# Weights of a two-layer decoder trunk: one 1 MB transfer for two neighbouring ring slots in place of two of 512 KB

## The reference, cut to what matters

```
for l in range(DEPTH):                       # DEPTH = 2
    h = _rmsnorm(x, attn_norm[l])
    x = x + _hybrid_mixer(h, ..., w_in[l], ..., w_kv_b[l], ..., w_branch[l], w_out[l])
    h = _rmsnorm(x, ffn_norm[l])
    gate, up = jnp.split(h @ w_gate_up[l], 2, axis=-1)
    x = x + (jax.nn.silu(gate) * up) @ w_down[l]
```

## Time and profile before

| what | value |
|---|---|
| median of three runs | 2885.08 us (2885.07 to 2885.09) |
| the profiled execution's own time | 2884.71 us |
| its span, first to last instruction | 2882.9 us |
| PE busy | 2875.4 us, 12964 matmuls |
| DVE busy | 1823.1 us |
| ACT busy | 1339.0 us |
| POOL busy | 648.2 us |
| transfers on SP's queue | 540.54 MB |

### The profile page before, as it was taken

How to read it: one execution, slowest core, us unless ns; L and a number is a source line. 1 busy time by engine, 2 the same in 40 slices (tenths; PEclk the granted TensorE clock), 3 DMA queues, 4 the chain that set the end, 5 groups by cost and what they waited for, 6 DMA issues and landing times.

```text
span 2882.9 us, 35147 instructions
## 1 busy us (share of the span) xinstructions
PE 2875.4 (100%) x12964; PEld 2381.4 (83%) x12964; DVE 1823.1 (63%) x2223; ACT 1339.0 (46%) x1570; POOL 648.2 (22%) x1033
## 2 busy tenths in 40 slices
PE   9999999999999999999999999999999999999999
PEld 8888888888888888888888888888888888888887
DVE  7589866687655555545575898656775555555554
ACT  5445554554444444444444455455544444344443
POOL 0025224144122312300000242231441213213000
PEclk9999999999999999999999999999999999999999
DMA  7666666775666666666666666666766666666665
GB/s 247 183 185 195 202 186 189 232 235 190 192 192 194 194 190 195 193 194 192 193 193 176 196 190 197 191 189 228 238 191 194 191 194 192 193 193 194 193 194 170
DMA packets 291293, 567.35 MB, mean 197 GB/s; under 512 B 18985, under 2 KB 24945, under 8 KB 291185
## 3 DMA queue, kind: packets, MB, share of 16 engines
q1 hardware_dynamic: 283888, 540.54, 61.9%
q10 hardware_dynamic: 7296, 25.44, 2.7%
HBM read 551.23 MB, written 14.68 MB: 196 GB/s over the span
## 4 chain that ended last, share of the span: by engine, by line
PE 94%; POOL 2%; DVE 2%; issue 1%; ACT 0%; DMA 0%; ACTq 0%; SPq 0%; DVEq 0%
PE acc L456 61%; PE acc L461 30%; POOL small L387 2%; PE acc L503 1%; DVE w_lo L1197 1%; PE acc L501 1%; DVE nat L1197 0%; DVE small L1197 0%; ACT w_hi L807 0%; PE acc L514 0%; PE acc L494 0%; PE acc L509 0%; DVE small L1215 0%; DMA w_raw<-in_w_in_dram 0%; PE acc L515 0%
## 5 line engine op out<-in xcount | busy, mean ns | idle before, releaser
L1197 DVE TENSOR_TENSOR w_lo<-w_raw,w_hi 128x1024 fp32r<-128x1024 f32 x1024 | 1259.9, 1234 | 1013.4 <-ACT w_hi L807 1008.8
L807 ACT ACTIVATE w_hi<-w_raw 128x1024 fp32r<-128x1024 f32 x1024 | 1084.5, 1060 | 1480.1 <-PE acc L461 1447.6
L456 PE MATMUL acc<-w_hi,opa_hi 128*128 128x512 f32 (+1 forms) x2364 | 930.7, 394 | 0.6 <-ACT w_hi L807 0.6
L456 PE MATMUL acc<-w_hi,opa_lo 128*128 128x512 f32 (+1 forms) x2364 | 918.0, 388 | 0.0
L456 PE MATMUL acc<-w_hi,opb_hi 128*128 128x512 f32 x1728 | 672.9, 389 | 0.1
L456 PE MATMUL acc<-w_hi,opb_lo 128*128 128x512 f32 x1728 | 672.3, 389 | 0.0
L461 PE MATMUL acc<-w_lo,opa_hi 128*128 128x512 f32 (+1 forms) x2364 | 629.3, 388 | 0.0
L456 PEld LDWEIGHTS acc<-w_hi,opa_hi 128*128 128x128 f32 x2364 | 444.0, 188 | 93.8 <-issue 6.4
L461 PEld LDWEIGHTS acc<-w_lo,opa_hi 128*128 128x128 f32 x2364 | 443.1, 188 | 90.9 <-DVE w_lo L1197 0.4
L456 PEld LDWEIGHTS acc<-w_hi,opa_lo 128*128 128x128 f32 x2364 | 444.1, 188 | 87.6
L461 PE MATMUL acc<-w_lo,opb_hi 128*128 128x512 f32 x1728 | 461.8, 389 | 0.0
(11 more groups left out here) (188 smaller groups left out, 1136.3 us busy)
## 6 DMA issues: line engine op xcount, KB each, us to landing
w_raw<-in_w_gate_up_dram SPq DMA_DIRECT2D x352, 512.0 KB, 4.4
w_raw<-in_w_in_dram SPq DMA_DIRECT2D x336, 512.0 KB, 3.7
w_raw<-in_w_down_dram SPq DMA_DIRECT2D x176, 512.0 KB, 4.4
w_raw<-in_w_branch_dram SPq DMA_DIRECT2D x64, 512.0 KB, 4.6
w_raw<-in_w_out_dram SPq DMA_DIRECT2D x64, 512.0 KB, 4.3
gate_store<-nat ACTq DMA_DIRECT2D x24, 512.0 KB, 3.8
arena<-gate_store ACTq DMA_DIRECT2D x24, 512.0 KB, 5.5
w_raw<-in_w_kv_b_dram SPq DMA_DIRECT2D x16, 512.0 KB, 4.3
```

The costliest lines, as they stand in the source:

```text
L456: pe.matmul(bank(pair, t, width), op[j][:, kt + k, t * P:(t + 1) * P], w_hi[:, s, k, 0:width], start=(first and k == 0 and j == 0), stop=F ...
L807: return act.activation(out, in_, ACT.Copy, scale=scale)
L1197: return dve.tensor_tensor(out, a, b, op)
```

## The change

After the first eight units, each load brings two units: for an even slot SP waits until both slots are free (`lo_ready` for the second of them, unit `m + 1 - 4`) and issues one transfer of 1 MB into both; for an odd slot it issues nothing. `hi` of either unit waits on the semaphore of the even slot. Nothing else is changed.

```
             def unit(n, m, w, l, u, col, width=N):
+                count = 1 if n + m < UB else 2
                 slot = m % RING
-
-                sp.wait_ge(lo_ready, lo_count(n, m - RING))
+                if slot % count:
+                    return
+
+                sp.wait_ge(lo_ready, lo_count(n, m + count - 1 - RING))
                 view, per = w
-                sp.dma_start(raw[:, slot:slot + 1, :, 0:width],
-                             view[:, l * per + u:l * per + u + 1, :, col:col + width]).then_inc(raw_landed[slot], 16)
+                sp.dma_start(raw[:, slot:slot + count, :, 0:width],
+                             view[:, l * per + u:l * per + u + count, :, col:col + width]).then_inc(raw_landed[slot], 16)
...
             def hi(n, nq, m):

                 s = m % RING
-                act.wait_ge(raw_landed[s], nq + 16 * (m // RING + 1))
+                alone = isinstance(n, int) and n + m < UB
+                act.wait_ge(raw_landed[s if alone else s - s % 2], nq + 16 * (m // RING + 1))
                 act.wait_ge(unit_done, n + (m + 1))
                 copy(w_hi[:, s], raw[:, s]).then_inc(hi_ready, 1)
```

## The result

| | median us | lowest and highest | runs |
|---|---|---|---|
| before | 2885.09 | 2885.07 to 2885.43 | 4 |
| after | 2920.24 | 2919.34 to 2921.22 | 4 |

The ratio is 1.0122, with an interval of 1.0109 to 1.0134: slower by 35.15 us, where 14.4 were forecast, and above the range. The profiled execution took 2921.22 us, 36.5 more than that of before.

A forecast was written before the change was run, and what follows sets the result against it. The prediction took PE's matmuls as the bound (busy 2875.4 of 2882.9 us). Terms 5.9 + 5.7 + 1.0 + 1.7 = 14.3 us on 2884.71 gave 2899.0, adjusted to 2899.4 and stated as 2899.5 us; range 2893 to 2916.

The forecast's parts named there:

- direction: Whole kernel: slower than 2890.9 us, given 0.90 over the cases; the forecast time was 0.50% slower.
- block 6: PE stops at `pair_scores`, waiting for copies queued behind late `hi` 56: 5.9 us in the first layer, 5.7 in the second.
- the steady state costs nothing: Projections, gate/up and down: 4.1 us of lateness meets 4.1 of landing cover and 6.9 more in the ring; PE loses nothing.
- matmuls held up by writes: Faster rival, 0.04: pairs free matmuls from transfers' writes, winning 24.6 us; against it, unit times stay 2.72 us throughout 400 us.
- The rival with more stops: Stops elsewhere, as in output projection transposes: 2909 to 2925 us, 10 to 25 beyond the 14.3 sum; chance 0.22.
- the ring has 11 us of cover: Argument against more stops: between 11 us of cover in the ring and 4.1 of lateness there is mostly room.
- the clock: PE's idling in block 6 may bring slow matmuls: 0 to 3.4 us, taken as 1.7 for one of two stops.
- The rule of the Trainium skill weighed there: Idle PE falls to half rate until busy again; by it both block 6 stops pay, 1.7 us more in the sum.
- The start: First pair, units 8 and 9, lands late and DVE has no pause until `lo` 12: 1.0 us, between 0.1 and 2.
- the smaller stop: Rival, 0.08: 1 MB lands as soon as 512 KB, block 6 stops 4.5 and 4.3 us; 2891 to 2894.5 us.
- The rate rule of the Trainium skill: SP's transfers: gather to 1 MiB or more for 75% of peak rate; the prediction answered that no rate is short here.

The follow-up runs named there:

- e5: Changed kernel with all pairs, but in block 6 ACT's three `pair_sb` copies stand ahead of `hi` of unit 56: 2915.81 us, 1.0107 to before.
- e3: Kernel before with the pair's later wait kept, each pair issued as two 512 KB transfers with semaphores of their own: 2909.51 us, 1.0082 to before.
- e4: Pairs only from unit 256 of each layer on (gate/up and down projections), the others loaded as before: 2885.20 us, 0.9999 to before.
- e10: Pairs only in units 184 to 223 of each layer (branches and first output projection block), single loads elsewhere: 2899.41 us, 1.0049 to before.
- e7: Changed kernel plus 48 unused 128-column matmuls on PE ahead of its block 6 wait in `pair_scores`, both layers: 2918.27 us, 1.0116 to before.
- e9: Kernel before with only units 56 and 57 of each layer paired, plus 48 unused matmuls ahead of PE's `pair_scores` wait: 2897.98 us, 1.0046 to before.
- e8: Changed kernel with units 56, 57 and 184 to 223 of each layer loaded singly, all other pairs kept: 2898.58 us, 1.0044 to before.
- e1: Changed kernel with only units 56 and 57 of each layer loaded singly again: 2912.91 us, 1.0093 to before.
- e12: Pairs only in units 58 to 183 of each layer (end of input projection, attentions), single loads elsewhere: 2894.77 us, 1.0034 to before.

## Why the prediction was wrong, and where it was right

**Right: direction, and block 6.** It named the chain SP, DVE, ACT, PE and put 5.9 and 5.7 us on it; the waits are 5.76 and 5.8. It added nothing for what comes behind them, and up to unit 183 only 0.6 us came, both layers together. Issue to `hi` was taken as 5.00 and took 4.94. e5 shows that the chain goes through the copies' place, e3 that the second half counts 1.2 of it.

**Right: the steady state costs nothing,** The earlier trace rows against e4. So does the argument against matmuls held up by writes.

**Wrong, the step that decided: the output projection was left out of the sum.** The rival with more stops, into whose 2909 to 2925 us the result falls, named it: the transposes at line 494 wait without cover, 0.8 us each, up to 4.1 more each. They waited 3.7 more each, with 3.9 of clock behind them, and e10 measures the part with all that hangs on it at 14.4 us. The argument against, that the ring has 11 us of cover, holds for `hi` on its way to PE. The merge doesn't stand in the ring. It stands on DVE behind a `lo`, at the end of a way through DVE, POOL, ACT and DVE, and a wait of 0.8 us says that this way had no cover. A link that already waits passes on all of a delay, and should have stood in the sum by the same working as `pair_scores`, at 2.72 + 1.36 each, giving 8 more. That this is near the 3.7 measured is in part luck: the lateness comes in a block earlier, at `lo` 208, and the loads there take longer than the working has (7.2 us from issue to `hi` 208).

**Wrong, a size: the clock.** Taken as 1.7 us for one of two stops, with 3.4 as the upper bound. The clock fell at all four stops. Block 6 alone lost 2.4 + 2.7 = 5.1, above the bound: I had taken what 3.78 us of matmuls at the start lost, but in the stretch at half the clock from 163.09 to 169.92 PE works for 5.2 us, and half of this is 2.6. How much is lost varies, from 1.4 to 2.7 us for a stop in after. The rule of the Trainium skill weighed there (TensorE: Matmul & The Clock Gate, "The two states you'll see") is borne out by this trace: when PE starts again after each stop of 4.5 to 5.8 us, the granted clock is at the lower level.

**Wrong, smaller sizes.** The start was 2.3 us, not 1.0; `hi` 8 started at 32.23, 0.2 us later than forecast once the 0.4 us that this execution lost before its first unit is taken off, so that pair came nearly as forecast. The step that failed is that DVE would have no pause from there to `lo` 12: `hi` of units 10 and 11 waited 4.21 us for the next pair and started at 38.44, DVE waited for it, and `lo` 12 started at 46.91, 3.5 us later than before's 43.42 where 1.3 were forecast. Beyond the stops 5.8 us came in small pieces, most of them in the branches, where I had none. And the range was said to begin at the lower end of the smaller stop, which that rival puts at 2891, not 2893; nothing hangs on it here.

**The sum again.** 11.6 (forecast 11.6) + 5.1 (1.7) + 2.3 (1.0) + 7.5 and 3.9 at line 497 (none) + 6.2 (none) = 36.6, against the profiled 36.5. Half of the miss, 11.4 of some 22 us, is the stop that was left out. The rate rule of the Trainium skill (DMA: Bandwidth & Descriptors, "Measured") points the right way for the rate, for the share of the queue fell by a tenth for the same bytes, but the rate had no say in the time.

**Left open.** Whether the stored gates on ACT's queue are why some loads of the branches took 6.1 to 8.1 us in place of 5.0: the two coincide in the trace, and no kernel moves the one without the other. Why the low clock lasted 6.8 us at three stops and 3.4 at the last. Why units 702 and 703 cost more when block 6 costs less (e7, e9), and what the slower executions of e5 and e7 lost beyond their profiles.

## What to carry to other kernels

Ask of a merged transfer not what its rate gains but which wait it moves: the first half is issued one period later and lands with the second, and in a ring that is otherwise full this reaches PE only where non-ring work stands in the queues behind a conversion. Find these places by the short waits that the critical engine already has, since a wait of under 1 us at one line means cover of zero, and put every such line into the sum with its own lateness and the clock behind it. Measure parts of a change alone and together before adding: a stop refills the buffers and hides what would be late behind it, so that removing it gives back less than its length.

## What the runs showed of the hardware

- 1 MB landed 5.0 us after issue in the median; 512 KB took 4.4 in gate/up and 3.7 in the input projection. A second half cost 0.6 us in the one and 1.3 in the other. In block 6 it cost 1.2 to 1.3 from issue to use.
- With some half a megabyte or more of another queue's transfers beside them, seven 1 MB loads took 6.1 to 8.1 us from issue to use; three without took 5.0 to 5.1.
- Idle times of PE of 4.5 to 5.8 us each came with 6.8 or 3.4 us at the lower clock, a loss of 1.4 to 2.7 us. 48 matmuls of 128 columns in place of the idle time kept it at 1.00 (e9). Shorter ones went either way: waits of 1.92 us (e5), 2.30 (e7), 2.73 (e3) and 2.87 (e8) came with such a stretch, waits of 2.13 (e1) and 2.48 (e12) with none.
- 6.4 points less of the queue's time for the same bytes (61.9 to 55.5%) moved the steady state by nothing in 400 us.
